# Stick-breaking weights by a scanned product with queries on partitions, and the differential norm's root on ScalarE

## What is computed

```python
# A, stick-breaking (z: scores of one head, strictly causal)
z = einsum('bhqd,bhkd->bhqk', q, k) * scale
mask = kpos[None, :] < qpos[:, None]
log1m = where(mask, log_sigmoid(-z), 0.0)
between = cumsum(log1m, axis=3, reverse=True) - log1m
a = where(mask, exp(log_sigmoid(z) + between), 0.0)
o_a = einsum('bhqk,bhkd->bhqd', a, v)
# B: q and k are normalised in groups of 32 columns
y = x * rsqrt(mean(x * x) + 1e-6)
```

## Time and profile before

| what | value |
|---|---|
| median of three runs | 828.03 us |
| profiled execution, its own time | 828.2 us |
| its span in the trace | 826.4 us |
| TensorE busy | 821.6 us, 99% |
| VectorE, ScalarE, GpSimd busy | 559.7, 477.8, 293.7 us |
| chain that ended last | PE 98%; DMA 1% |

### The profile page before, as it was taken

One profiled execution on the slowest core, in us unless ns is written; L12 is line 12 of the kernel. 1 busy time (PEld: TensorE's weight loads), 2 busy tenths in 40 slices (PEclk: granted clock), 3 DMA queues, 4 the chain that ended last, 5 costly groups with the idle time before them and its releaser, 6 DMA issues.

```text
span 826.4 us, 11044 instructions
## 1 busy us (share of the span) xinstructions
PE 821.6 (99%) x4050; PEld 673.7 (82%) x4050; DVE 559.7 (68%) x821; ACT 477.8 (58%) x715; POOL 293.7 (36%) x297
## 2 busy tenths in 40 slices
PE   9999999999999999999999999999999999999998
PEld 5888888888888888888888888888788888888886
DVE  5576889868865666655454688898697666666542
ACT  6886655785465554543457775567844645454441
POOL 0078784404303432320000889653061044323100
PEclk9999999999999999999999999999999999999999
DMA  9745877684558777785565556878745687877652
GB/s 332 271 138 178 222 230 219 182 247 131 203 178 229 199 230 212 223 221 183 167 203 195 162 192 192 224 222 210 223 153 178 206 214 218 230 223 212 215 184 71
DMA packets 119637, 167.76 MB, mean 203 GB/s; under 512 B 56608, under 2 KB 59040, under 8 KB 119328
## 3 DMA queue, kind: packets, MB, share of 16 engines
q1 hardware_dynamic: 119296, 166.79, 66.9%
q10 hardware_dynamic: 288, 0.27, 0.1%
HBM read 153.40 MB, written 1.05 MB: 187 GB/s over the span
## 4 chain that ended last, share of the span: by engine, by line
PE 98%; DMA 1%; issue 0%; SPq 0%; ACT 0%; DVE 0%
PE acc L732 91%; PE att L812 1%; PE att L895 1%; PE att L779 1%; PE att L886 1%; DMA w_raw<-in_w_in 1%; PE att L804 1%; PE acc L812 1%; PE att L853 0%; PE att L869 0%; PE att L908 0%; PE att L972 0%; PE att L963 0%; PE att L854 0%; PE att L839 0%
## 5 line engine op out<-in xcount | busy, mean ns | idle before, releaser
L1234 DVE TENSOR_TENSOR w_lo<-w_raw,w_hi 128x1024 fp32r<-128x1024 f32 (+1 forms) x276 | 365.4, 1337 | 147.1 <-ACT w_hi L996 144.6
L732 PE MATMUL acc<-w_hi,xt 128*128 128x512 f32 (+1 forms) x1728 | 432.3, 392 | 0.5 <-ACT xt L1019 0.3
L996 ACT ACTIVATE w_hi<-w_raw 128x1024 fp32r<-128x1024 f32 (+1 forms) x275 | 286.1, 1051 | 168.7 <-PE acc L732 159.1
L732 PEld LDWEIGHTS acc<-w_hi,xt 128*128 128x128 f32 x1728 | 319.0, 188 | 66.3 <-issue 1.3
L732 PE MATMUL acc<-w_lo,xt 128*128 128x512 f32 (+1 forms) x864 | 229.9, 388 | 0.0
L732 PEld LDWEIGHTS acc<-w_lo,xt 128*128 128x128 f32 x864 | 162.0, 188 | 32.9
L1485 POOL TENSOR_SCALAR small<-small 128x2 f32<-128x2 f32 (+4 forms) x14 | 10.4, 745 | 209.2 <-ACT sq_dump L1096 132.4
L1617 POOL COPY hid_t<-hid_halves_t 128x512 uint16<-128x512 uint16 x44 | 37.7, 885 | 94.3 <-DMA hid_halves_t<-hid_halves 80.0
L1608 POOL COPY hid_halves<-hid 128x512 uint16<-128x512 uint16 x44 | 45.6, 1064 | 65.2 <-DVE hid L1311 65.2
L1625 POOL TENSOR_TENSOR merged<-merged,prod 128x1024 f32<-128x1024 f32 x10 | 32.5, 3250 | 61.2 <-DVE prod L1283 60.3
L732 PE MATMUL acc<-w_hi,ht_hi 128*128 128x512 f32 x176 | 47.7, 390 | 0.0
(11 more groups left out here) (175 smaller groups left out, 723.5 us busy)
## 6 DMA issues: line engine op xcount, KB each, us to landing
w_raw<-in_w_ffn SPq DMA_DIRECT2D x88, 512.0 KB, 4.2
w_raw<-in_w_gate SPq DMA_DIRECT2D x64, 512.0 KB, 3.9
w_raw<-in_w_ffn_down SPq DMA_DIRECT2D x44, 512.0 KB, 4.0
w_raw<-in_w_in SPq DMA_DIRECT2D x39, 512.0 KB, 4.7
w_raw<-in_w_branch SPq DMA_DIRECT2D x16, 512.0 KB, 4.1
w_raw<-in_w_out SPq DMA_DIRECT2D x16, 512.0 KB, 3.3
bg<-in_b_gate SPq DMA_DIRECT2D x8, 512.0 KB, 5.4
w_raw<-in_w_in SPq DMA_DIRECT2D x8, 396.0 KB, 3.4
```

Source lines behind the costliest of these rows:

```text
L732: return pe.matmul(acc[bank0 + t][:, 0:N], x_part[:, k0 + k, t * P:(t + 1) * P], w_part[:, k, 0:N], start=first, stop=last)
L996: act.activation(w_hi[:, n % WR, :, 0:N], w_raw[:, n % RAW, :, 0:N], copy).then_inc(s_hi, 1)
L1234: dve.tensor_tensor(w_lo[:, n % WR, :, 0:N], w_raw[:, n % RAW, :, 0:N], w_hi[:, n % WR, :, 0:N].bitcast(F32), ALU.subtract).then_inc(s_lo, 1)
```

## The change

Mixer A is computed with queries on partitions. TensorE computes the scores of both pairs in slot 9 (step sm A; the second pair goes to the idle pair of product banks). VectorE adds the strict mask into eb. In slot 10 ScalarE makes the sigmoid of -z (into za) and of z (into eb), each over 4 heads by 384 columns. VectorE scans za backwards along the keys with a running product that starts anew at two columns (sscan, slots 11 and 12), and multiplies (smul, slots 12 and 13). GpSimd deals (slot 13, both pairs), SyncE turns (slots 21 and 22), ScalarE joins into za (slots 18 and 20), and pv moves to slot 27. The steps z, sp, cum and the mask matmuls go. Deals of A have transpose buffers of their own.

The root of prep B moves from GpSimd to a step brs (ScalarE, slot 14): Ln of the mean square plus epsilon, then Exp with scale -0.5, one after the other. GpSimd waits for it inside prep B.

Besides: the constants grow from 960 to 1216 columns and the masks' load goes; lambda moves to slot 15, the first Bpv to 29, the copy of A's output to 28; the transpose of kcs becomes a matmul with an identity on a cleared buffer of 128 partitions; two more memsets at the start. RANK loses the entries of Acum and Asp and gains none. Cut to its core:

```diff
-C_ID, C_TRI, C_ONE, C_R32, C_R64, C_CM, C_CZ, C_RC, C_REP, C_MK, C_END = 0, 128, 256, 384, 416, 480, 512, 544, 576, 704, 960
+C_ID, C_RS, C_R32, C_R64, C_CM, C_CZ, C_RC, C_REP, C_MK, C_END = 0, 128, 512, 544, 608, 640, 672, 704, 832, 1216
...
-TURNS = [("C", 0), ("C", 1), ("D", 0), ("D", 1), ("D", 2), ("D", 3)]
-TURN_P = (43, 47, 52, 53, 55, 56)
+TURNS = [("A", 0), ("A", 1), ("C", 0), ("C", 1), ("D", 0), ("D", 1), ("D", 2), ("D", 3)]
+TURN_P = (21, 22, 43, 47, 52, 53, 55, 56)
...
-    "stats": 1, "stats_f": 3, "lambda": 14, "x": (0, 0, 1, 2), "f": (-2, -1, 2, 3), "m": (-1, -1, 2, 3),
-    "sig": (49, 53, 57, 57), "o": (22, 45, 48, 58), "subln": 40, "prep": (13, 18, 25), "ngate": 25, "Aq": 6,
-    "Ak": 7, "Az": (9, 14), "Asp": (9, 14), "Acum": (13, 17), "Apv": (21, 21), "Bq": 19, "Bk": 20,
-    "Bsm": (21, 21, 27, 27), "Bp": (21, 24, 27, 29), "Bpt": (24, 27, 29, 32), "Bpv": (27, 29, 33, 35), "Bo": 36,
+    "stats": 1, "stats_f": 3, "lambda": 15, "x": (0, 0, 1, 2), "f": (-2, -1, 2, 3), "m": (-1, -1, 2, 3),
+    "sig": (49, 53, 57, 57), "o": (28, 45, 48, 58), "subln": 40, "prep": (13, 18, 25), "ngate": 25, "Aq": 6,
+    "Ak": 7, "Asm": (9, 9), "ssig": 10, "sscan": (11, 12), "smul": (12, 13),
+    "Apdeal": (13, 13), "brs": 14, "Apjoin": (18, 20), "Apv": (27, 27), "Bq": 19, "Bk": 20,
+    "Bsm": (21, 21, 27, 27), "Bp": (21, 24, 27, 29), "Bpt": (24, 27, 29, 32), "Bpv": (29, 29, 33, 35), "Bo": 36,
...
-        for n in range(PAIRS[mixer] if mixer != "A" else 0):
-            put(PLAN[mixer + "sm"][n], "sm", (mixer, n))
         for n in range(PAIRS[mixer]):
-            for kind in {"A": ("z", "sp", "cum", "pv"), "B": ("p",)}.get(mixer, ("p", "pdeal", "pjoin", "pv")):
-                put(PLAN[mixer + kind][n], kind, n if mixer == "A" and kind != "pv" else (mixer, n))
+            for kind in {"A": ("sm", "pdeal", "pjoin", "pv"), "B": ("sm", "p")}.get(mixer, ("sm", "p", "pdeal", "pjoin", "pv")):
+                put(PLAN[mixer + kind][n], kind, (mixer, n))
...
+    for n in range(2):
+        put(PLAN["sscan"][n], "sscan", n)
+        put(PLAN["smul"][n], "smul", n)
+    for kind in ("ssig", "brs", "lambda", "subln", "ngate", "cbuild", "ck", "cv", "cks", "kcprep", "kct", "cr", "cs", "cp", "cpt", "cpv"):
...
+        def p_buffer(k):
+
+            return k if k < 2 else 2 + k % 2
...
-                if kind == "z":
-                    for b in (S0, S1):
-                        pe.matmul(att[:, b, :].rearrange("p (s c) -> p s c", c=P)[:, 0:3:2, :], ident16,
-                                  mask_a.unsqueeze(1).to_broadcast([P, 2, P]), start=True, stop=False, skip_group_check=True)
                 if mixer == "B":
                     score_matmuls(l, sum(todo, []))
                 else:
                     for maps in todo:
-                        score_matmuls(l, maps, swap=kind == "z")
-
-            def cumulate(l, step):
-
-                pe.wait_ge(dve_misc.sem, dve_misc.at(l, ("sp", step[1])))
-                for h in range(2):
-                    for i in range(2):
-                        b, part = S0 + h, sp_parts[:, h, i, :]
-                        pe.matmul(att[:, b, 0:384], tri_r[:, 0, :], part, start=False, stop=False, skip_group_check=True)
-                        mm = pe.matmul(att[:, b, P:2 * P], tri_r[:, 1, :], part[:, 256:384], start=False, stop=i == 1,
-                                       skip_group_check=True)
-                mm.then_inc(att_done.now(step), 1)
...
-                            pe.transpose(att[:, TP, 0:16], kcs[:, :, :], ident[0:16, 0:16]
-                                         ).then_inc(att_done.now(step), 1)
+                            pe.matmul(att[:, TP, 0:16], kcs[:, :, :].rearrange("p m d -> p (m d)"), ident[:, 0:16],
+                                      start=True, stop=True).then_inc(att_done.now(step), 1)
...
-                elif kind == "z":
-
-                    act.wait_ge(att_done.sem, att_done.at(l, step))
-                    e_free(act, l, step)
-                    for f, kw in ((ACT.Abs, {}), (ACT.Exp, {"scale": -1.0}), (ACT.Ln, {"bias": 1.0})):
-                        ins = act.activation(zt1, att[:, S0:S0 + 2, 0:384] if f == ACT.Abs else zt1, f, **kw)
-                        ins.then_inc(s_zc, 1)
-                        softplus_chain[0] += 1
-                        if f != ACT.Ln:
-                            act.wait_ge(s_zc, softplus_chain[0])
-
-                elif kind == "cum":
-                    act.wait_ge(att_done.sem, att_done.at(l, step))
-                    pb = pt_free(l, step)
-                    act.activation(ptb[:, pb:pb + 2, :], att[:, S0:S0 + 2, 0:384], ACT.Exp
-                                   ).then_inc(read_act.now(step), 1)
-                elif kind == "sm":
+                elif kind == "ssig":
+                    act.wait_ge(read_dve.sem, read_dve.at(l, ("sm", ("A", 1))))
+                    act.activation(za[:, :, :], eb[:, :, :], ACT.Sigmoid, scale=-1.0).then_inc(s_zc, 1)
+                    act.wait_ge(s_zc, l + 1)
+                    act.activation(eb[:, :, :], eb[:, :, :], ACT.Sigmoid).then_inc(act_misc.now(step), 1)
+                elif kind == "brs":
+                    act.wait_ge(dve_misc.sem, dve_misc.at(l, ("prep", "B")))
+                    n = NT * 2 * MIX // DD
+                    if l == 0:
+                        act.wait_ge(s_init, 6)
+                    act.activation(rs[:, 0:n], ss[:, 0:n], ACT.Ln, scale=1.0 / DD, bias=epsb[:, 0:1]).then_inc(s_brs, 1)
+                    act.wait_ge(s_brs, l + 1)
+                    act.activation(rs[:, 0:n], rs[:, 0:n], ACT.Exp, scale=-0.5).then_inc(act_misc.now(step), 1)
+                elif kind == "sm" and a[0] != "A":
...
+                    if a[0] == "A":
+                        dst = za[:, 2 * a[1]:2 * a[1] + 2, :]
+                    else:
+                        pb = pt_free(l, step)
+                        dst = ptb[:, pb:pb + 2, :]
                     for i in range(2):
-                        ins = act.activation(ptb[:, pb + i, :].bitcast(U16).rearrange("p (c s) -> p s c", s=2),
-                                             p_halves_t[k % 2][:, i, :, :], copy)
+                        ins = act.activation(dst[:, i, :].bitcast(U16).rearrange("p (c s) -> p s c", s=2),
+                                             p_halves_t[p_buffer(k)][:, i, :, :], copy)
...
-                elif kind == "sp":
-
-                    dve.wait_ge(s_zc, 3 * (l * PAIRS["A"] + a + 1))
-                    settled(dve.scalar_tensor_tensor(out=zt2, in0=att[:, S0:S0 + 2, 0:384], scalar=0.0, in1=zt1,
-                                                     op0=ALU.max, op1=ALU.add))
-                    hi, lo = (sp_parts[:, :, i, :] for i in range(2))
-                    settled(dve.tensor_copy(hi, zt2))
-                    dve.tensor_tensor(lo, zt2, hi.bitcast(F32), ALU.subtract).then_inc(dve_misc.now(step), 1)
+                elif kind == "sm" and a[0] == "A":
+                    dve.wait_ge(att_done.sem, att_done.at(l, step))
+                    if l == 0:
+                        dve.wait_ge(s_const, 16)
+                    e_free(dve, l, step)
+                    for i in range(2):
+                        e, bank = e_of(step)[0][i], score_bank(l, step, i)
+                        dve.tensor_tensor(eb[:, e, 0:P], bank[:, 0:P], strict_add[:, 1, :], ALU.add)
+                        ins = dve.tensor_tensor(eb[:, e, P:384].rearrange("p (b k) -> p b k", k=P),
+                                                bank[:, P:384].rearrange("p (b k) -> p b k", k=P), strict_add, ALU.add)
+                    ins.then_inc(read_dve.now(step), 1)
+                elif kind == "sscan":
+                    dve.wait_ge(s_zc, l + 1)
+                    for h in (2 * a, 2 * a + 1):
+                        ins = dve.tensor_tensor_scan(out=za[:, h, ::-1], data0=za[:, h, ::-1], data1=restart[:, ::-1],
+                                                     initial=0.0, op0=ALU.mult, op1=ALU.max)
+                    settled(ins)
+                elif kind == "smul":
+                    dve.wait_ge(act_misc.sem, act_misc.at(l, ("ssig", None)))
+                    h = slice(2 * a, 2 * a + 2)
+                    dve.tensor_tensor(eb[:, h, 0:383], eb[:, h, 0:383], za[:, h, 1:384], ALU.mult
+                                      ).then_inc(dve_misc.now(step), 1)
...
-                            settled(rsqrt(rs[:, 0:n], ss[:, 0:n], d, half[:, 0:n]))
+                            if a == "B":
+                                pool.wait_ge(act_misc.sem, act_misc.at(l, ("brs", None)))
+                            else:
+                                settled(rsqrt(rs[:, 0:n], ss[:, 0:n], d, half[:, 0:n]))
...
-                            pool.wait_ge(dve_misc.sem, dve_misc.at(l, ("p", a)))
+                            if a[0] == "A":
+                                pool.wait_ge(dve_misc.sem, dve_misc.at(l, ("smul", a[1])))
+                            else:
```

(52 more changed lines are left out.)

87 lines of the change are left out of this document (33 added, 54 removed).

## The result

The changed kernel takes 846.21 us, the median of 4 runs (843.62 to 850.02), against 827.98 for the kernel before (827.73 to 828.12) on the same chip: ratio 1.0223 [1.0183, 1.0263]. It is slower by 18.2 us where I said 9.6, and above the top of my range. The profiled run is the fastest of the four, 843.62 us with a span of 841.8, 15.4 more than before. It therefore shows 15.4 us of loss, and 2.6 us up to the median must be something that the other runs have more of.

A forecast was written before the change was run, and what follows sets the result against it. TensorE, busy 821.6 of 826.4 us, was taken as the bound. Per layer, 8.0 us of new waits less 3.2 saved lose 4.8, 9.6 in two: 828.2 + 9.6 = 837.8, stated as 837.6, range 832.5 to 842.

The forecast's parts named there:

- Behind slot 24 ScalarE's next due item: ScalarE's copies for NSA's gate, slot 25: done about 2 us ahead of TensorE, so no further loss after chunk 24.
- I cost these at nothing: Lambda, B's first P times V and the copy of A's output move to later slots, instructions unchanged: no cost.
- the sum: Per layer, waits of 8.0 us less 3.2 us of work taken from TensorE: 4.8 lost, 9.6 in two layers.
- rival 3: The 5.9 us wait before Bk's transposes slows TensorE's clock; four later chunks show 5 us a layer: 848 us, chance 0.10.
- the rival's own words on chunk 20: At the slow clock chunk 20 takes 2 us more, free because chunk 24 waits for ScalarE.
- The order on GpSimd: In slot 13 prep B (rank 0.5) runs before A's deals (default 4), so the deals end only at 62.7 us.
- the chain to T: Mask, sigmoids, scans, norm reduction, root, prep B, deals and transpose in turn, up to the transpose's landing at 67.7 us.
- T: Moment in layer 0 when mixer A's transpose lands, forecast 67.7 us; a layer's net loss is this minus 62.9.
- the scans' length on the path: VectorE's four scans, 0.85 us each, stand ahead of the differential norm's reduction, which then ends at 48.5 us.
- my low bound: Scans at 0.47 us each instead of 0.85 would make the transpose land 1.5 us earlier.
- Rival 1: Clean gain without new waits, 821.8 us, needing the transpose landed before 59.7 us; chance 0.13.

## Why the prediction failed, and what of it held

**The step that failed** is "Behind slot 24 ScalarE's next due item ... is done about 2 us ahead of TensorE, so nothing more is lost", with "I cost these at nothing" for the first P times V of B and the copy of A's output. The former looked at slot 25 only. The latter held that an unchanged instruction costs the same in a later slot. It does, but a bank is held until its reader is done: the copy moved from 79.4 to 101.7, 22 us, behind the next set of eight exponentials, and the next writer of OB moved only from 90.1 to 101.6. The runs showed a wait of 2.3 us a layer there, 4.65 in all, in place of the nothing of the sum; moving Bpv by two slots took it away and, with the new waits of 1.4, gained 3.4 between profiled runs. It also let the clock fall in some executions, which is the next point.

**The clock** (rival 3) fell, but I had its place and its size wrong. Within the 5.56 us wait it fell to 0.50, at 69 us, and stood there until nearly 76; chunk 20 took 4.0 us in place of 2.3. Filling that wait won nothing, as the rival's own words on chunk 20 said. Nothing was lost on further chunks. The cost came behind the shorter wait of 2.3 to 2.7 us, where TensorE has no slack: 1.6 to 3.1 us each time, in some executions. With 4.65 and the 2.6 to the median, the miss of 8.6 us is explained to within 1.4: 1.2 are chunk 24's 0.6 us a layer below, and 0.2 because I took the profiled run to stand above the median. That the long wait brought the level of 1.2 GHz agrees with the Trainium skill, "TensorE: Matmul & The Clock Gate", section "HAM oscillation". That the clock also fell, in some executions, at waits less than half as long is not in that section, and here the traces decide; why the price came there and not behind the long wait follows from slack.

**What held.** The order on GpSimd (prep B, then the deals; the rank alone took the wait away) and the chain to T, by its terms, layer 0, predicted and measured: mask added 36.3 and 36.6; sigmoids 39.4 and 39.6; scans 0.85 and 0.90 each; reduction ended 48.5 and 48.6; root 50.3 and 50.8; prep B's body 10.2 and 11.3; deal of pair 0 done 62.7 and 64.0; T 67.7 and 67.8; Bk 71.3 and 71.4, a wait of 5.9 and 5.6; chunk 24 83.8 and 84.4. The 1.3 us by which the deal came late were made good by the first turn, which was on its way at 63.97 and landed 3.8 us later, where I had 5.0. That T came out so near is in part luck. The 0.6 us at chunk 24 came in between Bq's copy and the split of chunk 23, 6.3 us (71.33 to 77.60) where I had 5.7: ScalarE waited there for a weight load, which stands behind the transposes on SyncE's queue and which my sum left out:

```profile
72.54 0.86 ACT L968 ACTIVATE w_hi<-w_raw 128x792 fp32r<-128x792 f32 x1 [1.21 <-DMA w_raw<-in_w_in]
```

**Half right.** I had the scans' length on the path. As a duration it was right, and 0.90 us for 384 columns, against 0.51 for a maximum of the same shape (1.8 times as long), bears out the Trainium skill's section "Datapath and trigger behaviour" ("DVE: opcode table, instruction layouts, handler registers and perf-mode slots") on half throughput. But the root waits for ScalarE's split and table load, so the scans had 0.3 us of slack at the root, and shorter ones could not have brought T down by the 1.5 of my low bound; what their length cost, 1.5 us in all, came through prep B's body instead.

**Rival 1** did not happen, but two moves of slots brought it near: 824.8 us against its 821.8.

## What to carry to other kernels

When steps are moved later in a hand-made order, list for each the buffer it holds and who writes that buffer next: the copy that frees a bank is paid where the next writer stands, and what else is due on its engine just ahead of it decides. Take a wait's price at the full clock only where the engine behind it has slack.

## What the runs showed of the hardware that I had not expected

- The granted clock fell to 0.50 at waits of 2.3 to 2.7 us, and not every time: of the same twelve products behind the same 2.3 us, one profile shows 1.52 us and another 2.79. In the version with the joins late it fell in both layers, and cost 1.6 us in one and 3.0 in the other. What makes the difference between executions stays open.
- GpSimd's body of prep B took 8.7 us in one place and 11.3 in another. The instructions that are longer are those beside VectorE's own: rotations of 0.46 and 0.29 us take 1.33 and 1.27 while VectorE's three splits (55.09 to 59.9) take 1.48 to 1.76 instead of 1.22. A multiplication of 64 columns on VectorE takes 1.94 us beside the body's first instruction, which takes 2.55; without the scans it is done before the body starts and takes 0.22, and the body's first instruction takes 1.93. So in these traces both engines are slower side by side; which of their instructions do this to each other is not worked out here.
- A table load stands ahead of the wait of its activation and so can be the whole of the activation's delay: at L1083 the input was there 0.3 us before the load's end.
